# Attention stage of a diffusion step: the order of values, scores and the output copy within a unit

## The reference

```python
def one_block(qi):                        # 128 queries of all 8 heads
    s = einsum('bqhmd,bkhmd->bhmqk', qi, k) * HEAD_DIM ** -0.5     # two maps, m = 0, 1
    p = softmax(s, axis=-1)
    a = p[:, :, 0] - lam * p[:, :, 1]
    return einsum('bhqk,bkhe->bqhe', a, v)
# context queries see the 256 context keys; latent queries see 256 cached + 1024 latent keys
# in the same layer, from the same normalised h:
proj = h @ w_in                           # its Hyena and gate columns are needed after attention
```

## Time and profile before

| | |
|---|---|
| Median of 3 runs | 3305.28 us (3299.79 to 3305.64) |
| Profiled execution, its own time | 3302.12 us |
| Its span (first to last instruction) | 3300.3 us |
| PE busy over the span | 2799.3 us (85%) |
| DVE, ACT, POOL busy | 1342.2 (41%), 852.4 (26%), 949.6 us (29%) |
| Mean granted clock of TensorE | 0.923 of full speed |
| Attention stage | 748 to 1577 us of the span |

### The profile page before, as it was taken

How to read it: one execution, slowest core, us unless ns; L and a number is a source line. 1 busy time by engine, 2 the same in 40 slices (tenths; PEclk the granted TensorE clock), 3 DMA queues, 4 the chain that set the end, 5 groups by cost and what they waited for, 6 DMA issues and landing times. The chain is left out here.

```text
span 3300.3 us, 37222 instructions
## 1 busy us (share of the span) xinstructions
PE 2799.3 (85%) x14954; PEld 2361.0 (72%) x14954; DVE 1342.2 (41%) x1750; ACT 852.4 (26%) x1344; POOL 949.6 (29%) x658
## 2 busy tenths in 40 slices
PE   4886399797999999999577839978399999999995
PEld 3765388686788878788465627867388888888884
DVE  4553699813555444334245452122521222122214
ACT  1111211103555444444211142111212111211121
POOL 1442478811111011100355402210423223322330
PEclk9978699898999999999788859989699999999997
DMA  3347277634221222210554564240011111111111
GB/s 111 112 163 242 103 219 242 202 112 147 82 97 48 96 96 86 103 37 29 213 197 148 178 266 160 104 174 13 26 44 38 34 38 39 38 38 38 38 38 64
DMA packets 103896, 350.84 MB, mean 106 GB/s; under 512 B 12536, under 2 KB 26361, under 8 KB 103450
## 3 DMA queue, kind: packets, MB, share of 16 engines
q1 hardware_dynamic: 75914, 241.61, 20.9%
q0 software_dynamic: 27856, 107.49, 9.8%
HBM read 254.16 MB, written 86.51 MB: 103 GB/s over the span
## 5 line engine op out<-in xcount | busy, mean ns | idle before, releaser
L284 PE MATMUL ml_b<-h_hi,ml_whi 128*128 128x512 f32 (+1 forms) x768 | 273.0, 355 | 50.5 <-POOL ml_wlo L2027 50.5
L284 PE MATMUL at_out<-h_hi,at_whi 128*128 128x512 f32 (+1 forms) x672 | 266.6, 397 | 13.1 <-POOL at_wlo L680 10.5
L285 PE MATMUL ml_b<-h_lo,ml_whi 128*128 128x512 f32 (+1 forms) x768 | 272.9, 355 | 0.0
L286 PE MATMUL ml_b<-h_hi,ml_wlo 128*128 128x512 f32 (+1 forms) x768 | 272.5, 355 | 0.0
L285 PE MATMUL ml_b<-ml_ulo,ml_whi 128*128 128x512 f32 (+1 forms) x768 | 272.4, 355 | 0.0
L284 PE MATMUL ml_b<-ml_uhi,ml_whi 128*128 128x512 f32 (+1 forms) x768 | 272.1, 354 | 0.0
L286 PE MATMUL ml_b<-ml_uhi,ml_wlo 128*128 128x512 f32 (+1 forms) x768 | 271.6, 354 | 0.0
L680 POOL TENSOR_TENSOR at_wlo<-at_raw,at_whi 128x1024 fp32r<-128x1024 f32 x28 | 66.0, 2356 | 670.3 <-ACT at_whi L780 670.3
L856 DVE TENSOR_REDUCE at_nmax<-at_s 128x1 f32<-128x1280 f32 (+1 forms) x160 | 196.8, 1272 | 145.2 <-PE at_s L732 145.2
L2027 POOL TENSOR_TENSOR ml_wlo<-ml_raw,ml_whi 128x1024 fp32r<-128x1024 f32 x64 | 159.4, 2492 | 329.7 <-ACT ml_whi L2000 329.7
L2096 DVE SCALAR_TENSOR_TENSOR x_x<-ml_b,all_mod,x_x 128x512 f32<-128x512 f32 (+1 forms) x192 | 127.2, 662 | 310.5 <-PE ml_b L286 310.4
(11 more groups left out here) (273 smaller groups left out, 6555.5 us busy)
## 6 DMA issues: line engine op xcount, KB each, us to landing
hy_tab<-in_hy_tab POOLq DMA_DIRECT2D x68, 512.0 KB, 5.4
ml_raw<-in_w_mlp SPq DMA_DIRECT2D x64, 512.0 KB, 3.3
flt_tab<-in_filt_tab POOLq DMA_DIRECT2D x44, 512.0 KB, 5.4
hd_wa<-in_w_adaT SPq DMA_DIRECT2D x32, 512.0 KB, 3.7
at_raw<-in_w_proj SPq DMA_DIRECT2D x28, 512.0 KB, 4.6
s_spec<-flt_ob POOLq DMA_DIRECT2D x44, 256.0 KB, 5.2
s_gatesT<-at_pad SPq DMA_DIRECT2D x16, 640.0 KB, 2.9
mg_gate<-s_gatesT SPq DMA_DIRECT2D x16, 640.0 KB, 5.3
```

What stands on the lines that cost most here:

```text
L284: pe.matmul(out, w_hi, x_hi, start=first, stop=False)
L285: pe.matmul(out, w_hi, x_lo, start=False, stop=False)
L286: return pe.matmul(out, w_lo, x_hi, start=False, stop=last)
```

## The change

Four places in `stage_attention`:

- In each PE iteration `values(u - 2)` comes ahead of `qk_maps(u)` and not behind it.
- In each ACT iteration `output(u - 2)` comes right behind `evacuate`, ahead of `weights` and of both exponentials; before, it stood between the two exponentials.
- At the start, POOL makes the low halves of the first two blocks of weights and then issues the loads of q and k of heads 0 and 1. Before, the loads of head 0 came first and those of head 1 between the two.
- At the start, SP issues the loads of the values of head 0 ahead of the load of the convolution weights.

```diff
             for j in range(2):
                 load(j)
+            load_v(0)
             sp.dma_start(cw[:], g.d["conv"]).then_inc(cw_in, 16)
-            load_v(0)
             load(2)
...
-            load_qk(0)
-            weights(0)
-            load_qk(1)
-            weights(1)
+            for j in range(2):
+                weights(j)
+            for h in range(2):
+                load_qk(h)
...
             for u in range(STEPS - 1):
+                if u >= 2:
+                    values(u - 2)
                 if u < ALL_UNITS:
                     qk_maps(u)
-                if u >= 2:
-                    values(u - 2)
                 project(2)
...
                 j = unit_split_at(u)
+                if u >= 2:
+                    output(u - 2)
                 if j is not None:
                     weights(j)
                 if u < ALL_UNITS:
-                    exp_map(u, 0)
-                if u >= 2:
-                    output(u - 2)
-                if u < ALL_UNITS:
-                    exp_map(u, 1)
+                    for m in range(2):
+                        exp_map(u, m)
```

## The result

| | before | after |
|---|---|---|
| Median, us | 3304.64 (6 runs, 3299.79 to 3307.95) | 3409.39 (6 runs, 3404.48 to 3415.07) |
| Ratio to before, 95% interval | 1 | 1.0318 [1.0304, 1.0332] |
| Span of the profiled execution, us | 3300.3 | 3409.3 |
| First scores of unit 0 to the start of unit 80, us | 792.1 | 893.4 |
| PE's waits for the copy of `o` / of transposes, us | 24.9 / 6.5 | none / 109.7 |

The forecast was 3407 us, in a range of 3385 to 3430. Of the 109.0 us by which the span grew, 101.3 lie between the first scores and unit 80. The other 7.7 us are outside the units, the largest part 5.0 us in the Hyena stage (288.3 to 293.3 us from its first to its last instruction), where nothing was changed; over all the profiles of this case that stage took between 286.5 and 293.3 us, and the cause is not known.

A forecast was written before the change was run, and what follows sets the result against it. PE's own list was taken to bound the kernel (PE busy 85%). Profiled 3302.1 us plus 89.7 (units), -0.3 (start) and 14.4 (clock) gave 3405.9; forecast 3407 us, 3.1% slower, range 3385 to 3430.

The forecast's parts named there:

- The chain and its number: Latent units 4 to 9: second group no earlier than 9.25 us after unit start; wide +56.6 us, narrow +36.0 us.
- Unit 2 and 3: Units 2 and 3 of each head: unit 2 gains 6.3 us wide, 1.5 narrow; unit 3 loses 3.1 us together.
- Unit 0, narrow: Two context units with narrow output: later chain, bounds 0 and +2.25 us each, taken as +0.9, +1.8 us together.
- The copy of `o`: ACT's copy ahead of the exponentials removes PE's wait before the first group; its place shortens the chain by 0.
- the three signs: Wrong if second group comes before 9.2 us, map 1's exponential starts earlier after scores, or clock falls in wide units.
- The start: POOL and SP at stage start: PE starts between 0 and -1 us, taken -0.3; head 0 loads hidden, 2.5 us spare.
- The clock: TensorE after 19 new long stalls: 12.7 falls by 1.5 us, four old falls go; +14.4 us, between -4.6 and +24.
- The rival in which the clock stays up: TensorE in the attention stage: few falls of the granted clock behind the new stalls; 3387 us, chance 0.2.
- The rival in which it falls in all latent units: TensorE in latent units, wide too: 56 stalls by 1.5 us instead of 12.7; 3471 us, chance 0.1.
- Faster: Second group in latent units: wait for `o` goes and the chain doesn't take over; 3277 us, chance 0.03.
- The last step of the sum: Whole kernel: from 3405.9 us, with the runs' median 3.2 us above the profiled execution, to a forecast of 3407 us.

The follow-up runs named there:

- the filler: The changed kernel plus twelve matmuls of 256 columns, never read, ahead of the second group of transposes in 19 narrow units 3 to 9; 3384.23 us, ratio 1.0243.

## Why the prediction was right

- **The chain and its number.** 7.00 us from first score to second group held in the narrow latent units 4 to 9 of every kernel that kept PE's old order and the old place of the copy of `o` there, and with values first 9.25 us were forecast and 9.24 measured. Wide latent units: +1.75 each (56.1 us over 32 in the profile with the filler, 56.6 forecast). Narrow ones without a fall: +2.15 (34.4 us, 36.0 forecast); what follows the second group in them takes 2.33 us instead of the 2.42 that I carried over.
- **Unit 2 and 3.** Unit 2: -10.0 us, of which 1.1 was a fall that is gone; forecast -7.8. I took the idle time of the table of waits, 1.26 us, as what is won, but it counts from a matmul's modelled end; start to start the unit won 1.44. In the narrow units 2 the wait moved to the values of the next unit, as forecast; they won 0.55 each, forecast 0.5. Unit 3, wide: +1.4 us, forecast +1.7.
- **Unit 0, narrow.** Forecast +0.9 each, measured +0.13. The short exponentials stand 0.45 us apart when nothing stands between, and the second group came at 5.1 us, not 5.8. The bound held, the value in it was off.
- **The copy of `o`.** In the chain its place was worth next to nothing, though not quite the 0 that I took. Of the three signs that I named for being wrong, one came in, by a small amount: the exponential of map 1 starts 4.96 us after the first score matmul instead of 5.04 (unit 27) to 5.09 (unit 26), and the chain is some 0.08 us shorter. The values ahead of it took 2.32 us and not 2.25, which hides this in the 9.24. The run with ACT's order alone shows why the early copy does no harm here: with values first the copy starts 2.4 us after the unit's start, ahead of the maxima; with scores first it starts 4.5 us after it and holds the exponentials.
- **The start.** Forecast -0.3; its own run can't tell that from nothing. In the profile after, q and k of heads 0 and 1 took longer to land than I took (the slowest 14.8 us at the median of two, 11.6 before). The start's own edit does it, since the run with that alone has 14.5 us; that the loads slow each other down because both heads' are now issued one after the other is likely, and no run separates it. The scores still started without a wait.
- **The clock.** Forecast 12.7 falls by 1.5 us; there were 13, by 1.6. Four of them reached far into the next unit. The estimate of four in six from the earlier trace rows gave the count, and that is luck in part: it came from one execution, and in the profile of the run with the start alone the clock fell behind five of the same six stalls. Nor does the share follow the length: 17 of 22 stalls of 2.4 us with PE's order alone, 6 of 18 of 2.55 us with ACT's alone. The rival in which the clock stays up is what the filler made of the kernel: 3384.2 us measured, 3387 forecast for that case. The rival in which it falls in all latent units didn't come: no wide unit had a stall of its own followed by a fall. What the Trainium skill says of short gaps that repeat (page "TensorE: Matmul & The Clock Gate", section "A second HAM failure mode: psum-queue depth-cycling") the trace bears out for stalls of 2.9 us, in 13 of 19 cases, and not for those of 1.5 us in wide units. I left the wide units out because no stall under 1.93 us had a fall; they had none, but 1.93 us is no limit, as the 6 falls in 19 behind 1.46 us with the copy between the exponentials show.
- **Faster.** That the chain had no 2.25 us to spare is shown by the experiments that shorten the chain: with its last link moved between the exponentials the second group comes 1.39 us sooner (unit 26, 7.85 instead of 9.24), with shorter maxima 0.75 us.

Sum by the profiles: 80.2 us of stalls in the filler's units, 21.1 us of clock, together the 101.3 us between first scores and unit 80. The forecast, split alike (the four old falls that go counted with the stalls), had 89.7 - 4.6 = 85.1 and 19.0 us. The two misses, too much for the stalls and too little for the clock, offset each other in part. Of the 4.9 us too much for the stalls, 1.6 are in the narrow latent units, 1.6 in unit 0, 1.1 in unit 2 and 0.5 in the wide latent ones.

The mechanism was right, while the closeness of the total, 3407 against 3409.4, owes something to luck. The units fell 2.8 us short of the forecast's 104.1, and the 7.7 us outside them had no term. The last step of the sum is also loose: 3405.9 and the 3.2 us by which the median lay above the profiled execution give 3409.1, not 3407.

## What to carry to other kernels

When two blocks of work on the busiest engine change places, ask which of them starts a chain on the other engines, and measure from that block's start to the point where the busy engine wants the chain's end; the time to spare there, here 0.48 us or less, is all that the swap may use. A wait that the table names is not yet time to be won: here 24.9 us of waits for one copy hid a second wait right behind it. And where TensorE has to stand, a stall cut short or filled can be worth more than its length, by the clock that it doesn't lose; here that was 1.6 us for each fall.

## What was not expected of the hardware

Stalls of equal length had different outcomes. Behind 2.86 us in unit 24 the granted clock stayed at 1.00, behind 2.85 us in unit 27 of the same profile it was 0.53 of full speed for 6.7 us:

```profile
1038.16 0.66 PE L746 MATMUL at_turn<-all_ident,at_a 128*128 128x128 f32 x4 [2.86 <-ACT at_aT L825]
...
1075.27 1.11 PE L746 MATMUL at_turn<-all_ident,at_a 128*128 128x128 f32 x4 [2.85 <-ACT at_aT L825]
```

```profile
1037.60:1041.00 3.40, 2.84 (x23) 2.67 (x24) 1.34 (x3) 2.13 (x6) 0.00 (x0) 1.00 0.02 5
1074.90:1081.60 6.70, 6.33 (x31) 6.33 (x32) 1.86 (x3) 3.19 (x6) 0.00 (x0) 0.53 0.01 4
```

The first cost nothing, unit 24 being 11.58 us long; the second made unit 27 13.14 and unit 28 13.76 us long, against 11.58 and 12.76, 2.6 us in all. What decides between the two is left open; the length of the stall alone does not, since 1.46 us was enough in 6 of 19 cases in one kernel and 2.86 us was not in 6 of 19 in another. And 228 matmuls that did nothing useful (12 in each of 19 units) took 25 us off the median, 3409.39 to 3384.23 (ratios to before 1.0318 and 1.0243).
